# Where the big SBUF buffers of a two-block fp32 kernel begin: gaps that put each at a multiple of 128 bytes

## The reference

```python
h = rms_norm(x, g_mix)
p = h @ w_in                                  # 2048 x about 7500
x = x + concat([dsa_mixer(p), rwkv7_mixer(p)]) @ w_out
h = rms_norm(x, g_ffn)
for e in range(16):                           # each token uses 2 of 16
    x = x + combine[:, e] * ((silu(h @ w_gate[e]) * (h @ w_up[e])) @ w_down[e])
h = rmsnorm(x, norm1_g)
p = h @ w_in_2                                # 2048 x 12288
merged = sum(gate[n] * (y[n] @ w_branch[n]) for n in range(3))
x = x + merged @ w_out_2
x = x + square(relu(rmsnorm(x, norm2_g) @ w_mlp_in)) @ w_mlp_out   # 2048 x 8192 x 2048
return rmsnorm(x, final_g)
```

## Time and profile before

| what | value |
|---|---|
| median of three executions | 3079.04 us (3075.49 to 3079.43) |
| the profiled execution, its own time | 3072.47 us |
| its span, first to last instruction | 3070.7 us |
| mean granted TensorE clock | 0.989 |
| busy: PE, VectorE (DVE), ScalarE (ACT) | 97%, 62%, 50% |
| matmul records | 22,088 |
| read from HBM | 574.93 MB, 189 GB/s over the span |

### The profile page before, as it was taken

How to read it: one execution, slowest core, us unless ns; L and a number is a source line. 1 busy time by engine, 2 the same in 40 slices (tenths; PEclk the granted TensorE clock), 3 DMA queues, 4 the chain that set the end, 5 groups by cost and what they waited for, 6 DMA issues and landing times.

```text
span 3070.7 us, 52890 instructions
## 1 busy us (share of the span) xinstructions
PE 2969.6 (97%) x22088; PEld 2647.7 (86%) x22088; DVE 1918.6 (62%) x2591; ACT 1532.8 (50%) x2132; POOL 160.6 (5%) x248
## 2 busy tenths in 40 slices
PE   8999999879899999999999999999999999999998
PEld 7888889767688887777899999999989989898996
DVE  6555555774777777877659954445665545555454
ACT  5455444454566666655543347754344434344443
POOL 0000000200000000000075500000000000000000
PEclk9999999989899999999999999999999999999999
DMA  6223223223588888887444444445555555555554
GB/s 234 97 97 111 101 107 111 83 92 118 222 319 316 322 321 306 320 299 270 154 165 162 152 156 173 167 171 215 187 184 199 187 190 192 186 186 192 187 185 150
DMA packets 81955, 582.46 MB, mean 190 GB/s; under 512 B 9024, under 2 KB 9280, under 8 KB 12480
## 3 DMA queue, kind: packets, MB, share of 16 engines
q1 hardware_dynamic: 79056, 566.45, 50.1%
q10 hardware_dynamic: 2672, 12.71, 1.1%
HBM read 574.93 MB, written 4.19 MB: 189 GB/s over the span
## 4 chain that ended last, share of the span: by engine, by line
PE 87%; DVE 9%; ACT 2%; issue 1%; DMA 0%; ACTq 0%; SPq 0%; DVEq 0%
PE PG L799 10%; PE PG L797 10%; PE PG L800 10%; PE PG L824 6%; PE PG L825 6%; PE PG L823 6%; PE PG L855 5%; PE PG L1234 4%; PE PG L1235 4%; PE PG L1236 4%; PE PG L856 3%; PE PG L857 3%; DVE ring_r L699 3%; PE PX L942 2%; PE PX L1286 1%
## 5 line engine op out<-in xcount | busy, mean ns | idle before, releaser
L699 DVE TENSOR_TENSOR ring_r<-ring,work_r 128x1024 fp32r<-128x1024 f32 x492 | 584.3, 1230 | 313.6 <-ACT work_r L692 312.3
L692 ACT ACTIVATE work_r<-ring 128x1024 fp32r<-128x1024 f32 x492 | 493.1, 1052 | 537.9 <-PE PG L800 291.1
L692 ACT ACTIVATE C_r<-ring 128x1024 fp32r<-128x1024 f32 x268 | 269.1, 1052 | 418.5 <-PE PG L800 294.8
L800 PE MATMUL PG<-YT_r,ring_r 128*128 128x256 f32 x1664 | 469.4, 282 | 0.0
L699 DVE TENSOR_TENSOR ring_r<-ring,C_r 128x1024 fp32r<-128x1024 f32 x268 | 319.9, 1235 | 213.5 <-ACT C_r L692 212.3
L800 PE MATMUL PG<-work_r,ring_r 128*128 128x256 f32 x1344 | 374.9, 279 | 0.0
L800 PEld LDWEIGHTS PG<-YT_r,ring_r 128*128 128x128 f32 x1664 | 315.7, 190 | 0.0
L857 PE MATMUL PG<-HT_r,ring_r 128*128 128x256 f32 x960 | 271.7, 283 | 0.0
L800 PEld LDWEIGHTS PG<-work_r,ring_r 128*128 128x128 f32 x1344 | 253.4, 189 | 0.0
L824 PE MATMUL PG<-ring_r,HT_r 128*128 128x512 f32 x624 | 246.7, 395 | 0.0
L797 PE MATMUL PG<-YT_r,C_r 128*128 128x256 f32 x832 | 237.8, 286 | 6.2 <-DVE ring_r L699 6.2
(11 more groups left out here) (649 smaller groups left out, 7146.5 us busy)
## 6 DMA issues: line engine op xcount, KB each, us to landing
ring<-weights SPq DMA_DIRECT2D x472, 1024.0 KB, 4.8
C<-weights SPq DMA_DIRECT2D x32, 1024.0 KB, 4.8
work<-weights SPq DMA_DIRECT2D x32, 1024.0 KB, 4.9
work<-xT SPq DMA_DIRECT2D x4, 512.0 KB, 7.5
XT<-x ACTq DMA_DIRECT2D x1, 2048.0 KB, 8.4
residual<-XT ACTq DMA_DIRECT2D x4, 512.0 KB, 3.0
XT<-residual ACTq DMA_DIRECT2D x1, 2048.0 KB, 11.9
result<-YT SPq DMA_DIRECT2D x8, 256.0 KB, 2.9
```

Of the source, the lines that this page charges most:

```text
L692: act.activation(w_high(u)[:, c], weights(u)[:, c], ACT.Copy).then_inc(w_hi, 1)
L699: dve.tensor_tensor(w_low(u)[:, c], weights(u)[:, c], w_high(u)[:, c].bitcast(F32), ALU.subtract).then_inc(w_lo, 1)
L800: last = pe.matmul(o, wl, high[:, k, :], start=False, stop=(n == kts - 1), skip_group_check=True)
```

## The change

Only places change. A tensor of 104 floats (`gap`, 416 bytes) is put ahead of the ring, gaps of 32 floats (128 bytes) ahead of HT, ahead of C and ahead of `work`, and the constants get 176 unused columns (zeros), 3072 in all, 12,288 bytes. The same gaps are left in every declaration of the memory. By 512 the ring then begins at 384, HT, YT and XT at 0, C and SQ at 128, `work` at 256: all at multiples of 128.

| buffer | by 512 before | by 512 after |
|---|---|---|
| ring | 480 | 384 |
| HT, YT, XT | 480 | 0 |
| C | 480 | 128 |
| SQ | 288 | 128 |
| work | 288 | 256 |

```diff
-                     ("iota", 128)]:
+                     ("iota", 128), ("unused", 176)]:
...
+        sb("gap", [P, 104])
+
+        GAPS = (32, 0, 0, 32, 0, 32)
+
+        def places(pieces):
             shapes = [("ring", [P, RING, UNIT]), ("HT", [P, KT, T]), ("YT", [P, KT, T]), ("XT", [P, KT, T]),
                       ("C", [P, NC]), ("SQ", [P, 4, T])]
             shapes += [(f"work{i}", [P, n]) for i, n in enumerate(pieces)]
+            spaced = []
+            for i, shape in enumerate(shapes):
+                spaced += [(f"gap{i}", [P, GAPS[i - 1]])] if 1 <= i <= len(GAPS) and GAPS[i - 1] else []
+                spaced.append(shape)
+            return spaced
+
+        def split_memory(kind, suffix, pieces):
             with ExitStack() as c:
-                return [c.enter_context(nc.sbuf_tensor(n + suffix, shape, kind)) for n, shape in shapes]
+                all_of_them = [(n, c.enter_context(nc.sbuf_tensor(n + suffix, shape, kind))) for n, shape in places(pieces)]
+                return [tensor for n, tensor in all_of_them if not n.startswith("gap")]
...
```

More of the change, by code:

```diff
@@ L337, in build @@
         ONEKA = sb("ONEKA", [P, 8])
-        def split_memory(kind, suffix, pieces):
+        sb("gap", [P, 104])
+        GAPS = (32, 0, 0, 32, 0, 32)
+        def places(pieces):
             shapes = [("ring", [P, RING, UNIT]), ("HT", [P, KT, T]), ("YT", [P, KT, T]), ("XT", [P, KT, T]),
@@ L344, in split_memory @@
             shapes += [(f"work{i}", [P, n]) for i, n in enumerate(pieces)]
+            spaced = []
[4 more added lines that the diff above has]
+        def split_memory(kind, suffix, pieces):
             with ExitStack() as c:
-                return [c.enter_context(nc.sbuf_tensor(n + suffix, shape, kind)) for n, shape in shapes]
+                all_of_them = [(n, c.enter_context(nc.sbuf_tensor(n + suffix, shape, kind))) for n, shape in places(pieces)]
+                return [tensor for n, tensor in all_of_them if not n.startswith("gap")]
         def split_places(kind, suffix, pieces):
-            shapes = [("ring", [P, RING, UNIT]), ("HT", [P, KT, T]), ("YT", [P, KT, T]), ("XT", [P, KT, T]),
-                      ("C", [P, NC]), ("SQ", [P, 4, T])]
-            shapes += [(f"work{i}", [P, n]) for i, n in enumerate(pieces)]
             with ExitStack() as c:
-                return [c.enter_context(nc.sbuf_tensor(n + suffix, shape, kind)) for n, shape in shapes][6:]
+                all_of_them = [(n, c.enter_context(nc.sbuf_tensor(n + suffix, shape, kind))) for n, shape in places(pieces)]
+                return [tensor for n, tensor in all_of_them if not n.startswith("gap")][6:]
         ring, HT, YT, XT, C, SQ, work = split_memory(F32, "", [WORK])
```

## The result

The change made the kernel slower by a fifth of a per cent: 3083.28 us (median of 20 runs, 3078.44 to 3086.62) against 3077.36 us for the kernel before on the same chip (20 runs, 3073.79 to 3080.01), ratio 1.0019 with a 95% interval of 1.0013 to 1.0026. The forecast was 2980 us and faster.

What follows compares the result with a forecast made beforehand. PE's step from matmul to matmul was taken to bound the kernel. A gain of 112.7 us, less 9.6 and 4.5 kept back, made 98.6 us: 2980 us on the median's scale, range 2895 to 3085.

Steps and rivals of the forecast that it cites:

- What bounds the kernel: Whole kernel: PE's step between matmuls decides, 11.3 ns over the columns' time per 256-wide matmul, 17.4 ns per 512-wide.
- Moving operand: All 16,896 full-rate matmuls: aligned starts save one rung of 6.67 ns each, 112.7 us.
- the ladder: PE's step times: columns alone (106.7 or 213.3 ns) plus whole rungs of 6.67 ns, the time of 16 columns.
- The other side: PE's steps: starts don't count, the new operand distances are bad ones; 37 us slower, 3116 us, chance 0.14.
- Best spacing already seen: PE's steps: only operand distance counts, new distances bring all to the lowest seen; 64 us less, 3015 us, chance 0.20.
- Nothing happens: PE's steps: excess comes from the weight load's timing, not place; 3079 us, give or take 6, chance 0.14.
- All excess goes: All full-rate matmuls: the whole 221 us excess vanishes, a tenth kept; 199 us less, 2880 us, chance 0.12.
- What keeps part of it: Gain held back: 9.6 us to new waits in the first stage, 4.5 us to loads in the expert stage.
- VectorE, ScalarE, DMA: Weight split's address effects counted as nothing, at most 107 us without cover; larger constants load 0.24 us before PE.
- Half clock: Sign in the half-clock stretch: steps of 512 columns still take 426.7 ns after the change.

Runs made afterwards that it cites:

- spaced: Kernel before, with gaps putting ring 192 and constants 64 bytes behind features (mod 256), odd units' high weights moved 64 bytes: 3029.11 us, ratio 0.9851.
- work_back: Changed kernel with one gap halved (32 to 16 columns), returning work to its old place relative to the constants: 3069.6 us against 3075.26, ratio 0.9980.
- aligned_old_distances: Kernel before with one 32-byte gap ahead of the ring, all starts at multiples of 64, distances unchanged: 3077.41 us, ratio 0.9998.

## Why the prediction was wrong

The measured 3083.28 us lies inside the stated range, 2895 to 3085 us, but by under 2 us and by luck: the upper end stood for no change, and the sum behind the range gave 2980.

*What bounds the kernel.* Right: PE's step decides. The dense steps give the time to within some us: 0.65 ns more over 11,300 steps, 7 us, for the 5.9 of the change, and 53 us less for the 46.2 of spaced.

*Moving operand.* This is the step that failed: "I take one rung per matmul, the piece that a start 32 bytes off a 64-byte boundary would touch in addition". Starts at multiples of 64 with old distances gave 0.9998, L60 and L92 took the same 15.36 us, and spaced is the fastest kernel with none of its buffers at a multiple of 64. The term is 0 instead of 112.7 us. 113.3 and 120.0 do lie one and two rungs over the columns' 106.7, but the 117.7 of the earlier trace rows lies on no rung, and TensorE alone fills the space between them (115.5, 116.6, 118.4, 119.2 ns): the ladder is not a law. The rung that all steps keep was put down to the one thing that all buffers had in common. In TensorE alone an excess of a rung or more stayed at every start and distance tried.

The rule that the prediction set against itself fits: the Trainium skill, "Advanced Engine Details and Errata", Memory Cachelines, gives SBUF 16-byte lines, by which 32-byte starts lose nothing; no run here began off a multiple of 16.

*The other side.* The mechanism of this rival was the right one: the start doesn't count, the distance does, and the new ones are worse. Its own signs came true: dense 256-wide steps of 118.90 ns, over 118, and 512-wide ones at 231.39, no lower. They were weak signs, since the trace of before, 118.23 and 231.37, meets them too, and 118.90 also lies between the 117 and 119 that were to mean that nothing happened; it is the two runs that part starts from distances that decide. Its price, 37 us "at worst", was six times too high, since it put every step at the worst value seen; the trace has a gain and a loss in it. Features in HT against the constants' place went from (0,0) to (128,128), 120.0 to 118.7, which the prediction had seen ("can hardly get worse by moving apart"); against high weights in work they went from (64,0) to (0,128), 117.8 to 119.1, which takes it back; and with features in work both kinds of unit rose, the even ones from 113.3 or 117.8 to 118.7, the odd ones from 117.8 to 119.1. work_back undid the last and the time fell below both.

*Best spacing already seen.* Right that 113.3 can be had nearly everywhere by distance, and its 3015 us was near what spaced reached, 3029. Wrong that distances of 128 and 256 give it. The argument against it, that for 512 columns equal places were the faster, was true (226.7 against 228.9 to 233.4 alone) and weighed little, since 512-wide steps changed by 0.02 ns.

*Nothing happens.* The time was within this rival's 3079 give or take 6, but its reason falls: equal work takes 113.3 or 120.0 by distance. One thing of it remains. In the first block of the last MLP the even units ran at 113.3 ns in the trace of before, at 117.8 in that of aligned_old_distances and at 113.3 again in work_back, all with (192,192); the odd ones ran at 117.8 in all three. A unit can have two paces, and neither its distances nor whether it begins at a multiple of 64 settles which.

*All excess goes.* No pair of distances came below 113.3.

The Trainium skill gives PE's streaming operand and its weight load a read port each ("TensorE: Matmul & The Clock Gate", What happens when you issue a matmul). The runs don't agree as far as time goes: with all other engines idle, the same 96 steps took 11.52 or 10.89 us by nothing but where the one operand lay relative to the other.

*What keeps part of it; VectorE, ScalarE, DMA.* With no gain there was nothing to keep. In spaced some 8 of the 53 us of the dense steps were lost, a share not far from that of the 14 held back for 113. The split's 1229 and 1051 ns bear out the zero for VectorE and ScalarE.

*Half clock.* As foretold, it stays at 426.7 ns: six steps of 512 columns in 2.56 us at the new places, as in the earlier trace rows. The last line is a window of that stretch, granted clock 0.50.

```profile
1306.81 0.63 PE L1244 MATMUL PG<-HT_r,work_r 128*128 128x512 f32 x1
...
1309.37 0.63 PE L1244 MATMUL PG<-HT_r,work_r 128*128 128x512 f32 x1
...
1307.50:1309.90 2.40, 2.40 (x7) 1.81 (x7) 1.18 (x2) 0.00 (x0) 0.00 (x0) 0.50 0.35 147
```

Open: what in the chip the distance acts on. That it is the two operands of TensorE is shown, since nothing else ran; why 256 bytes are the period, why (64,192) is good, and what sets the pace where one pair has two, isn't.

## What to carry to other kernels

Before buffers are aligned, look at what the aligned places do to the distance between the operand that is loaded and the one that streams: here the alignment was worth nothing and the distance, modulo 256 bytes, up to 6.7 ns in 120. Measure a table of distances with TensorE alone, in the kernel's own order of operands and more than once, and then place buffers by it: 128 floats of gaps and two shifted starts gave 1.5%. Of a ladder of step times, the rung that no place has ever lacked is no forecast of what another place will give.

## What was not expected of the hardware

- The step of back-to-back fp32r matmuls with TensorE alone is 117.3 to 120.0 ns for 256 columns and 226.7 to 233.4 for 512 at single distances, 113.3 to 120.0 in threes; it repeats with 256 bytes of distance.
- The table for 256 columns and the one for 512 have their best places apart: (0,0) is the worst for the one (120.0) and the best for the other (226.7).
- A pair of distances can have two paces, 113.3 and 117.8 for (64,64), 118.6 and 120.0 for (128,128), 115.5 and 118.4 for (96,160); in the kernel the even units of a whole block, all with (192,192), ran at 113.3 or at 117.8.
- A stationary operand of 64 columns at distance 0 gave 113.3 ns for 256 streaming columns, one of 128 columns 120.0 and one of 32 columns 117.8.
